# Two heads' keys per PSUM bank, and row spreads by transposition, in a diffusion trunk's kernel

## The chip, the cores and the metric

The kernel runs on one core of one Trainium2 chip. The metric is the device time of one execution in microseconds; before the change three runs took 2082.91, 2083.75 and 2087.36 us, median 2083.75. Everything is float32.

## What is computed

One inference step of a hybrid trunk of two layers, over 512 latent tokens and 128 context tokens, width 1024. A layer is, cut to what matters here:

```
h = rms_norm(x) * (1 + sc1) + sh1
u, vg, ca, cg, rq, rk, rv, rgf, rgb, cq, ckv, kpe = split(h @ w_in)
y_a = spatial gating(u, vg)
y_b = silu(layer_norm(depthwise_conv(ca * sigmoid(cg)), g, b)) @ w_pw      # 256 channels
y_c = bidirectional retention(rq, rk, rv, rgf, rgb)
k, v = ckv @ w_ukv (per head 64 columns of keys, 64 of values) ; k = [k, kpe]   # 4 heads, 768 keys
y_d = softmax(q k^T) v
x = x + g1 * (concat(y_a, y_b, y_c, y_d) @ w_out)
x = x + g2 * expert_choice_ffn(rms_norm(x) * (1 + sc2) + sh2)              # 16 experts
```

g1 and g2 are vectors of 1024 gates, one pair for the latent and one for the context tokens; sc, sh and g come from `silu(c) @ w_mod`.

## The kernel before

Each engine has its program written out by hand and they meet at semaphores. A list STEPS gives the order of the steps of a layer, the same for all engines: input projections of 256 columns each (`in:...`), between them quarters of the modulation product (`mod:...`), latents, queries and keys of the attention (`latents`, `mla_q`, `mla_kv`), the convolution's statistics (`conv_mean`, `conv_var`, `conv_out`), 17 attention blocks (`att:...`), the gates' rows (`rows_g1`), retention, output projection, the choice of tokens by the experts, `rows_g2`, and then the loop over the 16 experts. There is no planner: an instruction stands where STEPS puts it, and waits there.

**PSUM jobs.** Results of TensorE go through three rings of two banks: wide (W, 1024 columns of float32), turned (T) and narrow (N). The lists W_JOBS, T_JOBS and N_JOBS hold the jobs of a layer in order, and a job's place in the list gives its bank (even or odd). `claim` makes TensorE wait until the job two places earlier has been read out, `finish` marks the job done, and `take`, on the instruction that read it out last, frees the bank. `wait` is the reader's wait for a job, `taken` the wait for its having been read out.

**Keys.** `mla_kv` on TensorE (L876 to L890) multiplies, for each of four heads, the head's 64 columns of w_ukv with the transposed latents ckvT of 768 keys, as 512 and 256 columns (L883, L884). The result uses partitions 0 to 63 of a wide bank and half the array's columns. ScalarE copies each head out in one instruction of 64x768 (the helper `out`, L1433, called in L1628) into khT. After the four heads come two jobs of values, v.0 and v.1 (L889), which claim the banks of kh.2 and kh.3; then `turn_q` transposes the queries (the helper `transposes`, L786). ScalarE's copies of v.0 and v.1 and of the turned queries follow the keys' in order, and then the projection `in:u` begins on TensorE (L827).

**Spreads.** In three places a column of values, one per partition, has to become a row that every partition holds. The kernel takes the column as weights, broadcast along the free dimension to 128x128, and multiplies it with the identity: each product gives 128 columns.

- `conv_var` (L914 to L927): five products at L926 spread the convolution's inverse deviation crstd over 640 tokens; VectorE multiplies with it (L1964), ScalarE applies SiLU (L1641) and only then does the softmax of the next attention blocks (L1532).
- `rows_g1` (L1021 to L1029): for latent and context tokens eight products each at L1028; ScalarE copies each 128x1024 job out (L1433). The last attention blocks follow: transposed probabilities of block 15 (L786), their copies by VectorE (L1997) and ScalarE (L1433), and the values (L990).
- `rows_g2` (L1205 to L1218): eight products at L1210 for the latent tokens' gates, then eight products of 32 columns at L1217 for the context tokens'. Ahead of them stand the small transpositions of the experts' tables (L1200, L1202); behind them a spare product (L1416) and the transposition of the first expert's rows (L1229), which POOL gathers from HBM with an indirect DMA (L2405) once the tables are out.

**Experts.** SP issues all weight loads. Each expert needs 12 MB of weights in a ring of 12 slots; expert 0 is loaded during the output projection, and a slot is loaded anew for expert 1 when TensorE has used it (semaphore s_gu_used, raised in `context_gate_up`, L1246).

The lines of a spread, as they stand in `rows_g1`:

```
for k in range(KD):
    ins = mm(o[:, k * P:(k + 1) * P], modT[:, 2 * KD + k, s:s + 1].broadcast_to([P, P]), ident, start=True, stop=True)
W.finish(ins)
```

The functions that the change touches:

Of the kernel before, what the change touches and what calls it, by code (L numbers as in the profile page):

```python
# [24 lines left out]
P = 128  # L25
D = 1024
KD = D // P
# [111 lines left out]
for _s in STEPS:  # L139
    _k, _, _a = _s.partition(":")  # L140
    if _k == "mod":
        for _w, _i in mod_steps(*map(int, _a.split("-"))):
            N_JOBS += [f"modc.{_i}"] if _w == "cols" else [mod_job(_i)] if mod_job(_i) else []
    elif _k == "modc":
        N_JOBS += [f"modc.{_a}"]
    elif _k == "norm1":
        W_JOBS += [f"{_k}.w{i}" for i in range(2)]
        T_JOBS += [f"{_k}.{i}" for i in range(4, KD + 2)]
    elif _k == "in":
        W_JOBS += ["mla_a.s", "mla_a.p", "mla_b"] if _a == "mla" else [f"{_a}.s", f"{_a}.p"] if _a in TOKEN_MAJOR else [f"{_a}.0", f"{_a}.1"]  # L150
        T_JOBS += ["ktok.0", "ktok.1", "ktok.p"] if _a == "rk" else []
    elif _k == "latents":
        T_JOBS += ["cq.0", "cq.1", "cq.p", "ckv.0", "ckv.1", "kpe.0", "kpe.1"]
    elif _k == "mla_q":
        W_JOBS += ["q.0", "q.1", "q.2"]
        T_JOBS += [f"qh.{h}" for h in range(HEADS)] + ["qh.p"]
    elif _k == "mla_kv":
        W_JOBS += [f"kh.{h}" for h in range(HEADS)] + ["v.0", "v.1"]
    elif _k == "mix":
        W_JOBS += ["mix.0", "mix.1"]  # L160
    elif _k == "conv_mean":
        W_JOBS += ["mean"]
    elif _k == "conv_var":
        N_JOBS += ["var"]
        W_JOBS += ["cstd"]
    elif _k == "conv_out":
        W_JOBS += ["pw.0", "pw.1"]
    elif _k == "att":
        W_JOBS += [f"s.{_a}"]
    elif _k == "rows_g1":  # L170
        W_JOBS += ["g1.s", "g1.p"]
    elif _k == "retention":
        N_JOBS += [f"kv.{t}" for t in range(NT)]
        N_JOBS += [f"rs.{_t}.{_h}" for _t in range(NT) for _h in range(2)]
        T_JOBS += [f"ro.{_t}.{_h}" for _t in range(NT) for _h in range(2)]
        T_JOBS += ["yc.0", "yc.1", "yc.p"]
    elif _k == "out":
        W_JOBS += [f"o.{_t}" for _t in (CTX, *range(TS))]
        T_JOBS += [f"xt.{_t}.{_h}" for _t in (CTX, 0, 1) for _h in range(2)] + ["afft.p"]
        T_JOBS += [f"xt.{_t}.{_h}" for _t in (2, 3) for _h in range(2)]  # L180
        N_JOBS += ["lg.p", "lg.s"]
    elif _k == "router_bias":
        N_JOBS += ["bias.r", "bias"]
    elif _k == "choose":
        T_JOBS += ["afft.s"]
    elif _k == "tables":
        T_JOBS += ["tables"]
    elif _k == "rows_g2":
        W_JOBS += ["g2.s", "g2.p"]
    if _k in ("att", "att_end"):  # L190
        for _i in [int(_a)] if _k == "att" else range(NBLOCK, ATT_STEPS):
            if weighed_at(_i) is not None:
                N_JOBS += [f"pv.{weighed_at(_i)}"]
            if turned_at(_i) is not None:
                T_JOBS += [f"pt.{turned_at(_i)}"] + ([f"pt.{turned_at(_i)}b"] if turned_at(_i) < NBLOCK - 1 else [])
# [136 lines left out]
def build(nc, io):  # L332
    ctx = ExitStack()
    with ctx:
# [397 lines left out]
        def _(pe):  # L732
# [143 lines left out]
            def mla_kv(l):  # L876
                wukv = par("wukv", HEADS, 2, NOPE)
                T.taken(pe, l, "ckv.0")
                T.taken(pe, l, "ckv.1")
                for h in range(HEADS):  # L880
                    W.claim(pe, l, f"kh.{h}")
                    o = bank(W, f"kh.{h}", NOPE)
                    mm(o[:, 0:512], wukv[:, h, 0, :], ckvT[:, 0:512], start=True, stop=True)  # L883
                    W.finish(mm(o[:, 512:NKEY], wukv[:, h, 0, :], ckvT[:, 512:NKEY], start=True, stop=True))  # L884
                for j, tiles in enumerate(((0, 1, 2, 3), (4, 5))):
                    W.claim(pe, l, f"v.{j}")
                    o = bank(W, f"v.{j}")
                    for n, t in enumerate(tiles):
                        ins = mm(o[:, n * GW:(n + 1) * GW].rearrange("p (h d) -> p h d", h=HEADS), ckvT[:, t * P:(t + 1) * P], wukv[:, :, 1, :], start=True, stop=True)  # L889
                    W.finish(ins)  # L890
# [23 lines left out]
            def conv_var(l):  # L914
                pe.wait_ge(s_csq, l + 1)
                N.claim(pe, l, "var")
                o = bank(N, "var")
                for t in range(NT):
                    for c in range(NG):
                        ins = mm(o[:, t:t + 1], csq[:, c, t * P:(t + 1) * P], mean_w[:, 0:1], start=(c == 0), stop=(c == NG - 1))  # L920
                N.finish(ins)
                pe.wait_ge(s_crs, l + 1)
                W.claim(pe, l, "cstd")
                o = bank(W, "cstd")
                for t in range(NT):
                    ins = mm(o[:, t * P:(t + 1) * P], crstd[:, t:t + 1].broadcast_to([P, P]), ident, start=True, stop=True)  # L926
                W.finish(ins)  # L927

            def conv_out(l):
# [91 lines left out]
            def rows_g1(l):  # L1021

                N.taken(pe, l, "modc.2")
                for s, job in ((1, "g1.s"), (0, "g1.p")):
                    W.claim(pe, l, job)
                    o = bank(W, job)
                    for k in range(KD):
                        ins = mm(o[:, k * P:(k + 1) * P], modT[:, 2 * KD + k, s:s + 1].broadcast_to([P, P]), ident, start=True, stop=True)  # L1028
                    W.finish(ins)  # L1029

            def retention(l):
# [173 lines left out]
            def rows_g2(l):  # L1205
                N.taken(pe, l, "modc.5")
                W.claim(pe, l, "g2.s")
                o = bank(W, "g2.s")
                for k in range(KD):
                    ins = mm(o[:, k * P:(k + 1) * P], modT[:, 5 * KD + k, 1:2].broadcast_to([P, P]), ident, start=True, stop=True)  # L1210
                W.finish(ins)
                W.claim(pe, l, "g2.p")
                o = bank(W, "g2.p")
                for j in range(QW // P):
                    for q in range(4):
                        col = modT[:, 5 * KD + q * (QW // P) + j, 0:1].broadcast_to([P, STRIP])
                        ins = mm(o[q * STRIP:(q + 1) * STRIP, j * P:(j + 1) * P], col, ident, start=True, stop=True)  # L1217
                W.finish(ins)  # L1218
# [209 lines left out]
        def _(act):  # L1428
# [132 lines left out]
            for l in range(DEPTH):  # L1561
                for s in STEPS:
# [61 lines left out]
                            src = bank(W, f"q.{j}").rearrange("p (t n) -> p t n", t=2)[:, 0:n, 0:HEADS * QK]  # L1624
                            out(W, l, f"q.{j}", qtok[:, 2 * j:2 * j + n, :], src)
                    elif kind == "mla_kv":
                        for h in range(HEADS):
                            out(W, l, f"kh.{h}", khT[0:NOPE, h, :], bank(W, f"kh.{h}", NOPE)[:, 0:NKEY])  # L1628
                        for j, n in enumerate((4, 2)):
                            out(W, l, f"v.{j}", vall[:, 4 * j:4 * j + n, :], bank(W, f"v.{j}")[:, 0:n * GW].rearrange("p (t n) -> p t n", t=n))  # L1630
                        for h in range(HEADS):
# [901 lines left out]
```

## Time and profile before

| what | value |
|---|---|
| runs | 2082.91, 2083.75, 2087.36 us |
| profiled execution, span | 2081.3 us |
| time around the span of that execution | not shown by the page |
| TensorE (PE) busy | 1946.8 us, 94% |
| TensorE weight loads (PEld) | 1084.3 us, 52% |
| VectorE (DVE), ScalarE (ACT), GpSimd (POOL) busy | 533.9, 450.5, 160.5 us |
| mean granted TensorE clock | 0.965 of full speed |
| HBM | 256 GB/s over the span, 380 to 398 in the expert slices |

The profile is of one execution. A float32 product stands in it as two MATMUL records (and two LDWEIGHTS), a transposition as one: L1028 has 64 records for 2 layers times 2 jobs times 8 products. A record's duration contains its way through the array, so the cost of one in a run of many is the length of the run divided by their number. Times are counted from the span's start; layer 0 goes to about 1050 us, layer 1 from there.

### The profile page before, as it was taken

The numbers are of one execution on the slowest core, as the hardware profiler recorded it, in microseconds if no ns is written. First come the engines' busy times: TensorE is split into PE (matmuls) and PEld (weight loads), VectorE is DVE, ScalarE is ACT, GpSimd is POOL, SyncE is SP. The second block draws the span as 40 slices with busy tenths as digits, with TensorE's granted clock in tenths as the row PEclk, the third lists the DMA queues.
The fourth block names the chain that finished last, engine by engine and source line by source line (L and its number), as shares of the span: only waits on it lengthen the run. The fifth ranks groups of instructions, "written<-read, shape, count | busy, mean of one in ns | idle before, by whom it ended". The sixth has DMA issues, their size and how long they took to land.

```text
span 2081.3 us, 36417 instructions
## 1 busy us (share of the span) xinstructions
PE 1946.8 (94%) x14936; PEld 1084.3 (52%) x14936; DVE 533.9 (26%) x1187; ACT 450.5 (22%) x947; POOL 160.5 (8%) x140
## 2 busy tenths in 40 slices
PE   4999999996999999999989999989699999999996
PEld 3756677882444434343365657778544344434342
DVE  1157123533101111111131932253511111111013
ACT  3132232221211111121132214332221121212112
POOL 0000001100111010101000000020010101111110
PEclk8999999996999999999999999999799999999998
DMA  8313122347999999999934122214559999999996
GB/s 311 102 43 122 41 82 85 115 169 271 381 385 395 388 390 393 389 394 390 398 132 139 41 83 81 81 62 194 214 211 392 390 393 389 394 386 397 385 397 240
DMA packets 172887, 532.98 MB, mean 256 GB/s; under 512 B 17296, under 2 KB 50192, under 8 KB 172560
## 3 DMA queue, kind: packets, MB, share of 16 engines
q1 hardware_dynamic: 155248, 493.53, 61.5%
q0 software_dynamic: 11712, 22.29, 4.9%
q10 hardware_dynamic: 5856, 16.16, 2.0%
q8 instruction: 52, 0.85, 0.2%
q14 instruction: 19, 0.16, 0.0%
HBM read 506.59 MB, written 25.33 MB: 256 GB/s over the span
## 4 chain that ended last, share of the span: by engine, by line
PE 66%; DMA 15%; SPq 9%; DVE 5%; issue 4%; ACT 1%; DVEq 0%; ACTq 0%
PE wide L1238 12%; DMA ring<-w_up 12%; PE wide L837 9%; PE wide L827 8%; SPq L644 7%; PE wide L1118 6%; PE wide L1246 6%; PE narrow L1269 6%; PE wide L1282 3%; DMA ring<-w_down 2%; PE turned L786 2%; PE narrow L758 1%; PE wide L954 1%; DMA ring<-w_mod 1%; PE narrow L990 1%
## 5 line engine op out<-in xcount | busy, mean ns | idle before, releaser
L1238 PE MATMUL wide<-ring,ht 128*64 128x512 f32 x2048 | 454.1, 599 | 9.4 <-DMA ring<-w_up 4.8
L1238 PEld LDWEIGHTS wide<-ring,ht 128*64 128x64 f32 x2048 | 143.6, 138 | 304.6 <-issue 278.3
L1269 PE MATMUL narrow<-ring,ht 128*64 128x512 f32 x1024 | 234.3, 599 | 2.3 <-DMA ring<-w_down 2.3
L1246 PE MATMUL wide<-ring,ht 128*32 128x256 f32 x4096 | 234.3, 380 | 0.0
L2202 DVE TENSOR_TENSOR ht<-ht,wide 128x512 f32<-128x512 f32 x64 | 35.5, 555 | 679.6 <-ACT ht L1760 459.2
L837 PE MATMUL wide<-stream,ht 128*128 128x256 f32 (+1 forms) x960 | 195.2, 365 | 3.5 <-DVE ht L1861 3.5
L837 PEld LDWEIGHTS wide<-stream,ht 128*128 128x128 f32 x960 | 171.3, 192 | 26.0 <-issue 5.0
L1246 PEld LDWEIGHTS wide<-ring,ht 128*32 128x32 f32 x4096 | 126.5, 110 | 108.2 <-issue 31.3
L827 PE MATMUL wide<-ht,stream 128*128 128x128 f32 (+1 forms) x640 | 176.3, 437 | 0.0
L1760 ACT ACTIVATE ht<-wide 128x512 f32<-128x512 f32 x32 | 19.1, 597 | 622.7 <-PE wide L1238 622.7
L2408 POOL DMA_INDIRECT moe_sums<-ht x60 | 93.3, 1554 | 712.2 <-DVE ht L2219 637.0
L827 PEld LDWEIGHTS wide<-ht,stream 128*128 128x128 f32 x640 | 96.9, 193 | 73.4 <-issue 73.4
L1269 PEld LDWEIGHTS narrow<-ring,ht 128*64 128x64 f32 x1024 | 67.6, 136 | 121.5 <-issue 114.4
L1282 PE MATMUL wide<-ring,ht 128*32 128x256 f32 x2048 | 117.6, 381 | 0.0
L1118 PE MATMUL wide<-stream,xn_yt 128*128 128x256 f32 x480 | 115.4, 397 | 1.6 <-ACT xn_yt L1499 1.6
L1433 ACT ACTIVATE ring<-wide 128x640 f32<-128x640 f32 (+7 forms) x56 | 40.1, 721 | 288.9 <-PE wide L837 158.7
L1118 PEld LDWEIGHTS wide<-stream,xn_yt 128*128 128x128 f32 x480 | 93.6, 199 | 15.3 <-ACT xn_yt L1433 2.1
L1936 DVE SCALAR_TENSOR_TENSOR ring<-ring,param_cols 128x670 f32<-128x670 f32 x120 | 99.4, 907 | 0.0
L1282 PEld LDWEIGHTS wide<-ring,ht 128*32 128x32 f32 x2048 | 63.1, 110 | 65.6 <-issue 27.5
L1752 ACT ACTIVATE ht<-turned,mod_cols,scale 128x64 f32<-128x64 f32 (+1 forms) x256 | 74.0, 393 | 7.2 <-PE turned L1229 6.7
L2219 DVE SCALAR_TENSOR_TENSOR ht<-narrow,ht 128x512 f32<-128x512 f32 x32 | 24.0, 751 | 185.3 <-PE narrow L1269 185.3
L2210 DVE TENSOR_SCALAR ht<-turned,scale,mod_cols 128x64 f32<-128x64 f32 (+1 forms) x256 | 60.9, 311 | 17.2 <-PE turned L1229 17.2
(283 smaller groups left out, 1549.9 us busy)
## 6 DMA issues: line engine op xcount, KB each, us to landing
ring<-w_gate SPq DMA_DIRECT2D x256, 512.0 KB, 12.3
ring<-w_up SPq DMA_DIRECT2D x256, 512.0 KB, 14.2
ring<-w_down SPq DMA_DIRECT2D x128, 1024.0 KB, 19.9
stream<-w_mod SPq DMA_DIRECT2D x38, 1024.0 KB, 5.4
stream<-w_in SPq DMA_DIRECT2D x20, 1024.0 KB, 7.4
ring<-w_mod SPq DMA_DIRECT2D x10, 1024.0 KB, 18.8
stream<-w_out SPq DMA_DIRECT2D x6, 1024.0 KB, 7.4
moe_sums<-x ACTq DMA_DIRECT2D x10, 512.0 KB, 5.5
```

Source lines behind the costliest of these rows:

```text
L644: sp.dma_start(ring[:, k, i, :], src.rearrange("l e p n -> (l e p) n")).then_inc(s_slot[k], 16)
L827: ins = mm(o[:, lo:hi], w[:, k, c * P:(c + 1) * P], hT[:, k, lo:hi], start=(k == 0), stop=(k == KD - 1))
L837: ins = mm(o[:, n * width:(n + 1) * width], src[:, k, t * P:(t + 1) * P], w[:, k, 0:width], start=(k == 0), stop=(k == KD - 1))
L1118: ins = mm(bank(W, f"o.{t}")[:, u * GW:(u + 1) * GW], yT[:, k, t * P:(t + 1) * P], out_weights[u][:, k, :], start=(u % 2 == 0 and k == OTH ...
L1238: ins = mm(psW[h * 64:(h + 1) * 64, 0, w * HALFW:(w + 1) * HALFW], xT[:, k, 0:CAPS], ring[:, k, w, h * HALFW:(h + 1) * HALFW], start=(k == ...
L1246: ins = mm(psW[q * STRIP:(q + 1) * STRIP, 1, w * QW:(w + 1) * QW], xT[:, k, CAPS:SLOTS], ring[:, k, w, q * QW:(q + 1) * QW], start=(k == 0 ...
L1269: ins = mm(psN[c * 64:(c + 1) * 64, 0, :], hmT[:, j, h_ * 64:(h_ + 1) * 64], ring[:, KD + k // 2, k % 2, c * HALFW:(c + 1) * HALFW], start ...
L1282: ins = mm(psW[q * STRIP:(q + 1) * STRIP, 1, HALFW:HALFW + QW], hmpT[:, j, q_ * STRIP:(q_ + 1) * STRIP], ring[:, KD + k // 2, k % 2, q * Q ...
L1752: ins = A(xT[:, k, lo:lo + n], bank(T, job)[:, k * GROWS + lo:k * GROWS + lo + n], ACT.Identity, scale=A2[:, k, s_:s_ + 1], bias=modT[:, 3 ...
L1936: ins = V.scalar_tensor_tensor(cacc[:, c, :], src, w[:, c, k:k + 1], cacc[:, c, :], ALU.mult, ALU.add)
L2210: ins = V.tensor_scalar(xT[:, 4 + k, lo:lo + n], bank(T, job)[:, k * GROWS + lo:k * GROWS + lo + n], A2[:, 4 + k, s_:s_ + 1], modT[:, 3 * ...
L2408: Q.indirect_dma_start(dst, bass.IndirectOffsetOnAxis(tables[:, j, e:e + 1], 0), src, None, compute_op=ALU.add).then_inc(s_added, 16)
```

## The change

Four edits. The keys of two heads go into one wide bank, head 2c in partitions 0 to 63 and head 2c+1 in 64 to 127, their products issued alternately; ScalarE reads each half out with an instruction of its own, the second into partitions 0 to 63. The three spreads with 128 output partitions are issued as transpositions of the broadcast column. The products of L1217 stay.

```diff
-        W_JOBS += [f"kh.{h}" for h in range(HEADS)] + ["v.0", "v.1"]
+        W_JOBS += [f"kh.{c}" for c in range(NG)] + ["v.0", "v.1"]
...
-                for h in range(HEADS):
-                    W.claim(pe, l, f"kh.{h}")
-                    o = bank(W, f"kh.{h}", NOPE)
-                    mm(o[:, 0:512], wukv[:, h, 0, :], ckvT[:, 0:512], start=True, stop=True)
-                    W.finish(mm(o[:, 512:NKEY], wukv[:, h, 0, :], ckvT[:, 512:NKEY], start=True, stop=True))
+                for c in range(NG):
+                    W.claim(pe, l, f"kh.{c}")
+                    o = bank(W, f"kh.{c}")
+                    for lo, hi in ((0, 512), (512, NKEY)):
+                        for f in range(2):
+                            ins = mm(o[f * NOPE:(f + 1) * NOPE, lo:hi], wukv[:, NG * c + f, 0, :], ckvT[:, lo:hi], start=True, stop=True)
+                    W.finish(ins)
...
-                    ins = mm(o[:, t * P:(t + 1) * P], crstd[:, t:t + 1].broadcast_to([P, P]), ident, start=True, stop=True)
+                    ins = nc.tensor.transpose(o[:, t * P:(t + 1) * P], crstd[:, t:t + 1].broadcast_to([P, P]), ident)
...
-                        ins = mm(o[:, k * P:(k + 1) * P], modT[:, 2 * KD + k, s:s + 1].broadcast_to([P, P]), ident, start=True, stop=True)
+                        ins = nc.tensor.transpose(o[:, k * P:(k + 1) * P], modT[:, 2 * KD + k, s:s + 1].broadcast_to([P, P]), ident)
...
-                    ins = mm(o[:, k * P:(k + 1) * P], modT[:, 5 * KD + k, 1:2].broadcast_to([P, P]), ident, start=True, stop=True)
+                    ins = nc.tensor.transpose(o[:, k * P:(k + 1) * P], modT[:, 5 * KD + k, 1:2].broadcast_to([P, P]), ident)
...
-                        for h in range(HEADS):
-                            out(W, l, f"kh.{h}", khT[0:NOPE, h, :], bank(W, f"kh.{h}", NOPE)[:, 0:NKEY])
+                        for c in range(NG):
+                            W.wait(act, l, f"kh.{c}")
+                            for f in range(2):
+                                ins = A(khT[0:NOPE, NG * c + f, :], bank(W, f"kh.{c}")[f * NOPE:(f + 1) * NOPE, 0:NKEY], ACT.Identity)
+                            W.take(ins, f"kh.{c}")
```

## Rows read from the trace of the kernel before

**Rows 1.** The page: busy us, share of the span, records
```profile
PE 1946.8 (94%) x14936; PEld 1084.3 (52%) x14936; DVE 533.9 (26%) x1187; ACT 450.5 (22%) x947; POOL 160.5 (8%) x140
```
**Rows 2.** The page: chain that ended last, by engine
```profile
PE 66%; DMA 15%; SPq 9%; DVE 5%; issue 4%; ACT 1%; DVEq 0%; ACTq 0%
```
**Rows 3.** Stretches of the expert loop: busy times, clock, DMA share, GB/s
```profile
520.00:730.00 210.00, 210.00 (x1942) 87.74 (x1936) 27.19 (x82) 36.42 (x88) 24.37 (x18) 1.00 1.03 387
```
**Rows 4.** The chain around layer 0's keys: start us, us, what
```profile
127.34 1.00 PE wide L883 x2
128.34 0.43 PE wide L884 x2
...
132.64 1.94 PE wide L889 x8
...
134.60 2.00 ACT ring L1433 x3
```
**Rows 5.** The chain in the expert loop, records and loads merged
```profile
571.84 13.88 PE wide L1238 x64
```
**Rows 6.** Timeline, layer 0: one of four copies of keys, ScalarE
```profile
128.81 0.80 ACT L1433 ACTIVATE ring<-wide 64x768 f32<-64x768 f32 x1 [0.94 <-PE wide L884]
```
**Rows 7.** The chain at transpositions, layer 1, and records of L798 (ns, minimum first)
```profile
1060.62 1.90 PE wide L798 x16
...
1067.40 1.94 PE turned L786 x8
...
L798 PE MATMUL wide<-const_cols,xn_yt x32: 272/375/447, 18.0 to 1062.2; 128*128 128x128 f32 x32
```
**Rows 8.** The chain and ScalarE's timeline around g1's spread, layer 0
```profile
336.69 3.77 PE wide L1028 x32
...
341.41 0.27 ACT L1433 ACTIVATE ring<-turned 128x128 f32<-128x128 f32 x1
341.78 1.31 PE narrow L990 x20
```
**Rows 9.** The chain at g2's spread, layer 1
```profile
1509.17 3.71 PE wide L1210 x16
...
1514.95 0.48 PE turned L1229 x4
```
**Rows 10.** Timeline and chain around crstd's spread, layers 0 and 1
```profile
230.07 1.79 PE L926 MATMUL wide<-const_cols,stats 128*128 128x128 f32 x10 [0.58 <-DVE stats L1962]
231.90 1.49 DVE L1964 TENSOR_TENSOR ring<-ring,wide 128x1280 f32<-128x1280 f32 x1 [1.89 <-PE wide L926]
237.62 2.35 PE L990 MATMUL narrow<-ring 128*64 128x128 f32 x20 [1.78 <-issue]
...
1253.92 1.66 PE wide L926 x10
```
**Rows 11.** Stretches of 1 us, clock third from last: a fall, two rises
```profile
230.00:231.00 1.00, 0.93 (x7) 0.93 (x8) 0.02 (x1) 1.00 (x1) 0.00 (x0) 0.94 1.09 388
...
234.00:235.00 1.00, 1.00 (x6) 0.78 (x6) 0.93 (x3) 1.00 (x2) 0.00 (x0) 0.85 0.00 0
...
1070.00:1071.00 1.00, 1.00 (x7) 0.60 (x5) 0.19 (x1) 0.47 (x2) 0.00 (x0) 0.72 0.00 0
```
**Rows 12.** The chain at g2's spread, layer 0
```profile
493.43 5.30 issue
498.73 1.32 PE turned L1229 x8
```
**Rows 13.** One tile: the gather of layer 1's first rows, POOL
```profile
L2405 POOL DMA_INDIRECT xn_yt<-moe_rows,ht x1: 957/957/957, 1511.0 to 1511.0; - x1
DMA to landing us min/median/max: 3.9/3.9/3.9
```
**Rows 14.** Stretches behind g1's spread, layers 0 and 1
```profile
340.00:347.00 7.00, 5.04 (x63) 4.19 (x62) 2.07 (x5) 2.04 (x5) 0.00 (x0) 1.00 0.34 113
...
1362.00:1371.00 9.00, 6.78 (x96) 5.74 (x97) 2.07 (x5) 2.52 (x8) 0.00 (x0) 1.00 0.27 89
```

## The prediction

> **What bounds the kernel now.** I read the page first for the balance, then the chain of waits for what ends last in each stage, and only then the stages that the change touches. The page says TensorE: busy for 94% of the span, no other engine above 26% [rows 1]. The chain agrees, 66% of it is TensorE, and adds 15% DMA and 9% SP's issues [rows 2]. These two lie in the expert loops. There the DMA engines are at a share of 1.03 while TensorE has no gap either [rows 3]: from the moment when expert 0 frees its first slots, the loop is the loading of a fixed number of bytes, and it ends a fixed time after that moment. So two questions decide what an edit is worth: does it bring TensorE's chain forward in the dense part of a layer, and does that reach the first product of expert 0? Between the keys and the experts I see transfers ordered by what TensorE has used, no idle DMA wait of TensorE, and VectorE's long convolution ending well ahead of its reader; a gain there should be handed on whole. Microseconds below are per layer unless said otherwise, and there are two layers.
>
> **Keys.** A head costs 0.86 us for 512 columns and 0.43 for 256, 1.29 together, the first 0.14 more [rows 4], and four heads 5.16. The two records of the 512 take 430 ns each although they use half the array's columns. In the expert loop the same form, issued for two halves alternately, gives 64 records of 512 columns (32 products) in 13.88 us, 217 ns each [rows 5]. So two halves do run beside each other, and two heads should cost 1.29: TensorE saves 2.58. ScalarE takes part of it back. It begins at 128.81 and needs some 0.74 for each of four copies (0.80 recorded [rows 6], less the overlap of neighbours), so it frees the bank of kh.0 at about 130.3; kh.1 is through at 130.06, so v.0 starts some 0.3 to 0.4 late. v.0 then takes 1.94 and ScalarE's copy of it starts at about 132.45 where it started at 134.60 [rows 4]. What follows (copies, turned queries, the next projection) is a chain behind that copy: **2.15 us** gained. Bounds: nothing, if the halves don't overlap (v.0's copy then starts where it did), and 2.58 if ScalarE were no limit. The copies from partitions 64 to 127 into 0 to 63 have no row; I price them like [rows 6], at worst double, which frees kh.0 0.8 later and costs that much of the 2.15. I take 2.15, since [rows 5] is the same form of product. Late next is ScalarE.
>
> **The price of a transposition.** Sixteen take 1.90 at full clock and eight 1.94 at half: 119 and 243 ns [rows 7] (the 16 stand behind products at full clock, the 8 behind idling). A spreading product takes 3.77/16 = 236 ns at full clock [rows 8] and 3.71/8 = 464 at half [rows 9]. A transposition is one record where the product is two, so half the price is what I expect. No row has a transposition with a broadcast operand; bounds are 119 and 236, and I take 119, as the products of [rows 8] read such columns at the speed of their two records.
>
> **crstd.** VectorE starts 1.83 after the first record in layer 0, and the run takes 1.66 in layer 1 [rows 10]. In layer 0 the clock fell from 2.4 to 1.2 GHz within the run: 0.94 over its first microsecond puts the fall at 230.9 [rows 11]. Five transpositions take 4 x 0.119 and the last one's record, 0.27 [rows 7]: 0.75, done ahead of such a fall. VectorE then starts 1.08 and 0.91 earlier. SiLU, the softmax and the values wait in line behind it: TensorE stands idle 1.78 us ahead of L990 [rows 10], so the gain passes on. **2.0 us for both layers**; bounds 0 at a product's price and 2.0.
>
> **g1.** TensorE: 16 x (236-119) = 1.87. The turned probabilities of the last block and their copy move with it; but ScalarE's second copy of gates (1.0 each for 1024 columns, by the 0.80 for 768 [rows 6]) now ends at about 339.7 and its copy of block 15 (0.27) at 340.0, and L990 needs that. It would start at 340.1 where it started at 341.78 [rows 8]: **1.7 us**. Late next is ScalarE again. Bounds 0 and 1.87.
>
> **g2.** Eight transpositions at half clock save 3.71-1.94 = 1.77 of TensorE's time [rows 7, 9], and I count nothing of it. In layer 0 TensorE waits 5.30 afterwards for the first expert's rows [rows 12]. In layer 1 the gather starts at 1511.0 and lands 3.9 later, 1514.9, and TensorE starts at 1514.95 [rows 9, 13]. The cover is the gather, released by the tables ahead of the spread; were it gone, 1.77 would be gained. There is even something to lose. In layer 1 L1229 runs at full clock (0.48 for four records, where eight took 1.32 in layer 0 [rows 9, 12]), behind the spread's activity; with a shorter spread and more idling it should run at half, and I put a **loss of 0.5 us** in layer 1. ScalarE's copies of these gates lie in the same cover.
>
> **Sum.** 2 x 2.15 + 2.0 + 2 x 1.7 - 0.5 = 9.2 us. The page gives the profiled execution's span alone, 2081.3; the runs' median is 2.5 above it, and I carry that over: 2072.1 of span, **2074.5** of time. The clock's falls between the keys and the experts lie where the work happens to be thin, and with every stage 2 to 7 us earlier they will lie otherwise. The spell of half clock that began at 230.9 ended at 234.3 (0.85 over that microsecond [rows 11]): 3.4 us, at most 1.7 lost or given back by one such spell; I allow 3 in all to each side.
>
> **A rule that speaks against it.** Behind g1's 16 products the clock stays at 1.00 [rows 14], and the rows say that transpositions can serve as well: in layer 1 a run of nothing but transpositions began at half clock [rows 7] and in its course the clock rose (0.72 over the microsecond from 1070 [rows 11], still within such a run). The Trainium skill's page "TensorE: Matmul & The Clock Gate", Part 4, says that transposes don't count as TensorE being busy, so that full clock does not engage for them. By that rule the spreads would stop holding the clock. By it the time would be the first rival's, 2077.9, and by the rows 2074.5. The trace doesn't agree: the rise in [rows 11] came with transpositions alone. No row tells whether they hold a clock as well as products do.
>
> **Rivals.**
>
> *Transpositions hold the clock less than products.* The clock falls behind g1's spread in both layers. For a spell as long as the one above, 3.4 us, what follows runs at half speed: L990 takes 2.35 as in [rows 10] for 1.31 [rows 8], the turned blocks and row sums some 0.7 more, 1.75 in all, as much as g1 gains. 2074.5 + 3.4 = 2077.9. For it: a stretch of 1.9 us of single records in place of 3.77 of double ones, and idling around it. Against: the rise of [rows 11]. Chance 0.17. The Trainium skill's page "TensorE: Matmul & The Clock Gate", Part 4, would have it so.
>
> *The halves of the array don't overlap for keys*, or ScalarE's shifted copies take the gain: 2074.5 + 4.3 = 2078.8. Against: [rows 5]. Chance 0.09.
>
> *A transposition of a broadcast column costs what the product does.* Then the change does only the keys: 2083.75 - 4.3 = 2079.5. Against: [rows 7]. Chance 0.08.
>
> *The clock falls with the first spread and stays down until the output projection*, and expert 0 starts cold: slower than before. Price: 5.04 us of TensorE's work behind g1 in layer 0 and 6.78 in layer 1 [rows 14], now at full clock, would take twice that, 11.8 more; one more spell at half clock at crstd and one at expert 0 in each layer, 4 x 1.7 = 6.8. Together 18.6 against 9.7 gained: 2083.75 - 9.7 + 18.6 = 2092.7. It decides from 9.7 us on, about 19 us more at half clock. The rise in [rows 11] speaks against it. Chance 0.04.
>
> **How the numbers follow.** My forecast has 0.62 and its own range is 2071.5 to 2077.5. To hold 8 in 10 the range takes in the weaker clock and most of the keys' rival: 2070.0 to 2080.0. A measurement of this kernel tells about 0.2% from no change, 4.2 us, so faster is below 2079.6 and slower above 2087.9. Faster: nearly all of the forecast (0.60), most of the weaker clock (0.14), half and more of the keys' rival (0.06) and less than half of the spreads' (0.03): 0.83. Slower: 0.04. Between: 0.13.
>
> **What would show it.** Keys: four records of 512 columns in about 0.9 us, where two took that, v.0's copy by ScalarE 5.1 us after the first key record instead of 7.3. Spreads: half the records, 0.6 us in crstd's and 1.9 in g1's, VectorE's L1964 0.8 after its first. L990 behind g1 3.4 after the spread's first record, where it was 5.1. Ahead of the experts only an idle wait that grew by 1.8 in layer 0, with the gather as its end. The expert loops as long as before, to 1 us. Wrong I would be if the granted clock behind g1 fell to 0.50 for such a spell or more, if the key records took 430 ns each, or if the expert loops changed their length.

## The result, and the profile after

Five runs of the changed kernel took 2071.93 to 2077.11 us, median 2073.98; the kernel before, on the same chip, had a median of 2082.91. The ratio is 0.9955 (95%: 0.9943 to 0.9967), which is 9.4 us less; the medians lie 8.9 apart. The forecast was 2074.5. The profiled execution took 2072.48 us, 2.2 of them around its span of 2070.3 (the forecast had carried over 2.5); the span before was 2081.3, so the two profiles lie 11.0 apart. Of the runs below, one execution of the keys alone took 4751.92 us, for no reason that the record shows, and its ratio leaves that one out. Lines in the changed kernel: keys L885, values L891, keys' copies L1632, crstd's spread L928, VectorE's product with it L1969, g1's L1030, g2's L1212, values of attention L992, first expert's rows L1231.

The page of the changed kernel, busy times and the chain by engine:

```profile
PE 1930.2 (93%) x14878; PEld 1070.2 (52%) x14878; DVE 533.8 (26%) x1187; ACT 450.6 (22%) x947; POOL 160.7 (8%) x140
...
PE 65%; DMA 15%; SPq 9%; DVE 5%; issue 4%; ACT 1%; DVEq 0%
```

TensorE has 58 records fewer and is busy 16.6 us less [rows 1]. That is more than the span lost, so part of its saving lies where nothing waits for it.

**Keys**, layer 0, timeline of TensorE, then of ScalarE (start us, us, engine, line, operation; in brackets the idle time before and its releaser):

```profile
124.38 2.80 PE L885 MATMUL wide<-ring,param_cols 128*64 128x512 f32 x16
127.62 2.86 PE L891 MATMUL wide<-param_cols,ring 128*128 128x256 f32 x12 [0.44 <-ACT ring L1632]
...
125.93 3.28 ACT L1632 ACTIVATE ring<-wide 64x768 f32<-64x768 f32 x4 [0.96 <-PE wide L885]
129.65 1.52 ACT L1435 ACTIVATE ring<-wide 128x1024 f32<-128x1024 f32 x2 [0.44 <-PE wide L891]
```

Sixteen records take 2.80 us from the first one's start to the last one's end, where four heads took 5.37 (5.16 without the way through the array of the last one [rows 4]): two halves run beside each other. TensorE then stands 0.44 for ScalarE, and v.0's copy begins 129.65 - 124.38 = 5.27 after the first key record, where it was 7.3. The four copies start 0.81 to 0.83 apart and last 0.80 to 0.81 each, those out of the upper half no longer than the others.

**crstd**, layer 0, timelines of TensorE and VectorE, and layer 1, TensorE:

```profile
226.78 1.22 PE L928 MATMUL wide<-const_cols,stats 128*128 128x128 f32 x5 [0.58 <-DVE stats L1967]
227.79 1.92 PE L956 MATMUL wide<-ring 96*128 96x512 f32 x2
...
228.03 1.49 DVE L1969 TENSOR_TENSOR ring<-ring,wide 128x1280 f32<-128x1280 f32 x1 [1.31 <-PE wide L928]
...
1247.54 1.33 PE L928 MATMUL wide<-const_cols,stats 128*128 128x128 f32 x5 [0.58 <-DVE stats L1967]
```

VectorE starts 1.25 after the spread's first record, not 0.8: the five transpositions ran at 1.2 GHz, or nearly all of them, in both layers. Stretches of the changed kernel, columns as in [rows 3] (the last three are granted clock, DMA share, GB/s):

```profile
227.00:228.00 1.00, 1.00 (x6) 1.00 (x5) 0.00 (x0) 0.80 (x1) 0.00 (x0) 0.50 1.10 391
1248.00:1249.00 1.00, 1.00 (x6) 1.00 (x5) 0.09 (x1) 0.57 (x1) 0.00 (x0) 0.50 1.09 386
```

The line's records say so too (minimum, median, maximum in ns):

```profile
L928 PE MATMUL wide<-const_cols,stats x10: 363/421/476, 226.8 to 1248.5; 128*128 128x128 f32 x10
L1030 PE MATMUL wide<-const_cols,mod_cols x32: 272/273/323, 332.7 to 1353.7; 128*128 128x128 f32 x32
```

The second line is g1's: a transposition's record lasts 273 ns at 2.4 GHz, and crstd's median of 421 is that of records at 1.2.

**g1**, layer 0, timelines of TensorE and ScalarE:

```profile
332.74 1.96 PE L1030 MATMUL wide<-const_cols,mod_cols 128*128 128x128 f32 x16
334.54 0.71 PE L786 MATMUL turned<-const_cols,ring 128*128 128x128 f32 x5
336.07 1.31 PE L992 MATMUL narrow<-ring 128*64 128x128 f32 x20 [0.82 <-DVE ring L2002]
...
333.87 1.94 ACT L1435 ACTIVATE ht<-wide 128x1024 f32<-128x1024 f32 x2 [2.50 <-PE wide L1030]
335.69 0.28 ACT L1435 ACTIVATE ring<-turned 128x128 f32<-128x128 f32 x1
```

L992 starts 3.33 after the spread's first record, where it was 5.16 by the same timeline (336.62 to 341.78). VectorE's copy of the turned block ends at 335.88, ScalarE's at 335.97: the two are level, and both bound what is left.

The first rival expected the clock to fall behind this spread. Stretches behind it, of the changed kernel in layers 0 and 1, then of the kernel before in layer 0:

```profile
336.00:343.00 7.00, 5.49 (x80) 4.68 (x81) 1.38 (x4) 1.22 (x5) 0.00 (x0) 1.00 0.37 116
1355.00:1369.00 14.00, 11.61 (x162) 9.72 (x162) 4.58 (x17) 3.17 (x12) 0.00 (x0) 1.00 0.25 74
...
343.00:357.00 14.00, 11.93 (x130) 10.10 (x127) 3.72 (x13) 2.92 (x10) 0.00 (x0) 0.64 0.05 13
```

The kernel before has a fall there itself, which [rows 14] just miss: from 346.9, 10.3 us behind the first record of its spread, it stands at 0.50 for 10.2 us. In the changed kernel the clock falls at 343.0, 10.3 behind the spread's first record too, and for 3.4 us only; in layer 1 the kernel before has a fall at 1370.9 and the changed one none. So behind g1 there is less half clock with transpositions, not more.

**g2**, chain of layer 0, then of layer 1 (start us, us, what):

```profile
481.35 1.90 PE wide L1212 x8
483.25 1.01 PE wide L1219 x16
484.26 0.52 PE narrow L1418 x2
484.78 6.80 issue
491.58 1.32 PE turned L1231 x8
...
1498.06 1.90 PE wide L1212 x8
1499.95 1.01 PE wide L1219 x16
1500.97 0.52 PE narrow L1418 x2
1501.48 2.18 issue
1503.67 1.31 PE turned L1231 x8
```

The spread is 1.8 shorter and the idle time behind it is 6.80 instead of 5.30 [rows 12], and in layer 1, where it was 0.54, 2.18. The gather sets L1231's start in both: in layer 1 POOL issues it at 1499.82 and it lands 3.8 later.

**All stages.** The table adds both layers of one profiled execution per kernel, from the first record of one stage to the first record of the next, in us. Those of the experiments stand here too, but for the two with drawn-out spreads. "keys" goes from the first key product to `in:u`, "conv" from the convolution's means to its variance, "crstd" from the spread to the next values (L992), "g1" from the spread to L992, "ret." from retention to the experts' tables, "in" from the first input projection to the keys. "dense" is the whole from the first input projection to the first expert's product, with stages that have no column; "loop" goes from there, in layer 0, to the first input projection of layer 1.

| kernel | in | keys | conv | crstd | g1 | ret. | dense | loop |
|---|---|---|---|---|---|---|---|---|
| before | 155.97 | 22.62 | 66.58 | 14.96 | 10.33 | 276.96 | 899.50 | 570.53 |
| after | 154.78 | 18.48 | 68.29 | 14.06 | 6.66 | 273.68 | 887.65 | 571.86 |
| the change again | 156.65 | 18.47 | 68.26 | 13.82 | 6.66 | 274.53 | 889.24 | 572.40 |
| keys alone | 159.05 | 18.48 | 68.20 | 14.27 | 10.34 | 274.05 | 896.17 | 572.63 |
| g1 alone | 157.77 | 22.62 | 66.57 | 14.52 | 6.66 | 274.81 | 893.10 | 572.20 |
| crstd alone | 157.84 | 22.61 | 66.57 | 13.04 | 10.33 | 270.64 | 891.29 | 573.03 |
| spreads alone | 158.02 | 22.62 | 64.94 | 13.61 | 6.67 | 271.44 | 887.08 | 573.00 |
| spreads again | 157.77 | 22.62 | 66.58 | 13.03 | 6.66 | 271.58 | 888.22 | 571.02 |
| g2 by products | 156.26 | 18.48 | 68.27 | 14.15 | 6.67 | 271.04 | 886.77 | 570.64 |
| keys in turn | 156.37 | 18.52 | 68.29 | 14.13 | 6.66 | 271.28 | 887.44 | 570.56 |
| time refilled | 159.06 | 22.67 | 64.94 | 13.02 | 6.66 | 272.09 | 888.17 | 570.22 |
| wide variance | 157.96 | 18.48 | 68.22 | 13.04 | 6.66 | 274.43 | 890.64 | 572.34 |

Read down a column: keys and g1 have two values each, to 0.05 us, and change with the edit alone. The others change with spells of half clock: conv is 32.47 a layer without one and 34.1 with one, and "in" of layer 0, which no edit can reach, is 76.64 in the changed kernel without half clock and 79.33 in the kernel before with 5.45 us of it. Of the 11.0 between the two profiles, keys give 4.14, g1 3.67 and crstd 0.90, together 8.7. The rest, 2.3, is the balance of the spells (in and ret. 4.5 less, conv 1.7 more, and smaller ones) and of the loop, 1.3 longer.

### The profile page after: what moved, and what is told of

It is laid out like the page before. It is cut to its first block, busy times and chain, and to the rows that moved or that the text cites. A ratio compares the mean times of both kernels' runs of the same rounds, so it can differ in the third digit from the quotient of the medians.

```text
span 2070.3 us, 36301 instructions
## 1 busy us (share of the span) xinstructions
PE 1930.2 (93%) x14878; PEld 1070.2 (52%) x14878; DVE 533.8 (26%) x1187; ACT 450.6 (22%) x947; POOL 160.7 (8%) x140
## 4 chain that ended last, share of the span: by engine, by line
PE 65%; DMA 15%; SPq 9%; DVE 5%; issue 4%; ACT 1%; DVEq 0%
PE wide L1240 12%; DMA ring<-w_up 12%; PE wide L837 9%; PE wide L827 8%; SPq L644 7%; PE wide L1248 6%; PE wide L1120 6%; PE narrow L1271 6%; PE wide L1284 3%; DMA ring<-w_down 2%; PE turned L786 2%; PE narrow L758 2%; PE wide L956 1%; DMA ring<-w_mod 1%; PE narrow L1143 1%
## 5 line engine op out<-in xcount | busy, mean ns | idle before, releaser
L1435 ACT ACTIVATE ring<-wide 128x640 f32<-128x640 f32 (+6 forms) x48 | 33.8, 708 | 277.5 <-PE wide L837 157.7
L1757 ACT ACTIVATE ht<-turned,mod_cols,scale 128x64 f32<-128x64 f32 (+1 forms) x256 | 74.1, 393 | 10.6 <-PE turned L1231 10.2
```

What stands on the lines that cost most here:

```text
L1757: ins = A(xT[:, k, lo:lo + n], bank(T, job)[:, k * GROWS + lo:k * GROWS + lo + n], ACT.Identity, scale=A2[:, k, s_:s_ + 1], bias=modT[:, 3 ...
```

## The experiments

Ratios are to the kernel before on the same chip, and gains in us are worked out from them; one per mille is 2.08 us.

**Keys alone.** The changed kernel with all three spreads as products.

```diff
-                    ins = nc.tensor.transpose(o[:, k * P:(k + 1) * P], modT[:, 5 * KD + k, 1:2].broadcast_to([P, P]), ident)
+                    ins = mm(o[:, k * P:(k + 1) * P], modT[:, 5 * KD + k, 1:2].broadcast_to([P, P]), ident, start=True, stop=True)
```

(and likewise for crstd and g1.)

> The change with its three spreads turned back into products: only the keys are paired. By my sum (the halves of the array work beside each other, ScalarE then limits) v.0's copy starts 5.2 to 5.3 us after the first key record instead of 7.3, and the time is 4.2 us below the kernel before, about half of what the change gives. By the rival that the halves don't overlap, or that ScalarE's copies from the upper partitions take the gain, it is within 1 us of the kernel before, and the change's gain is the spreads' alone.

Measured: 2079.0 us over 12 runs (2078.46 without that one), 0.9982 (0.997 to 0.9993). The stage is 2.07 shorter in each layer, and the total is shorter by 3.7, with an interval of about 2.4 to each side.

**Spreads alone.** The kernel before with the three transpositions and its own keys; run twice, the second time beside a repeat of the whole change.

```diff
-                    ins = mm(o[:, t * P:(t + 1) * P], crstd[:, t:t + 1].broadcast_to([P, P]), ident, start=True, stop=True)
+                    ins = nc.tensor.transpose(o[:, t * P:(t + 1) * P], crstd[:, t:t + 1].broadcast_to([P, P]), ident)
```

(and likewise for g1 and g2.)

> The kernel before with the three spreads as transpositions and its keys as they were. By my sum 2.0 (crstd, both layers) + 3.4 (g1) - 0.5 (g2) = 4.9 us below the kernel before, or 4.1 with crstd's run at half clock as the changed kernel's trace has it. Together with the keys alone this should add up to the whole change's 9. By the rival that transpositions let the clock fall behind g1's spread, 1 to 2 us below.

Measured: 2072.37 us, 0.9946 (0.9933 to 0.9959).

> The kernel before with the three spreads as transpositions, again. The stage from the convolution's mean to its variance takes 32.5 us in one layer at least (no spell at half clock), and the stage from crstd's spread to the next values 6.5 at full clock or 7.0 to 7.1 at half.

Measured: 2072.97 us, 0.9951 (0.9936 to 0.9967).

> The changed kernel unaltered, beside the spreads alone on one chip. By the sum of the stages (keys 2.07 us a layer) it is 4.1 us below the spreads alone. By the theory that the keys' gain is partly given back, because with the work 2 us earlier a spell at half clock (1.6 us) falls between the convolution's mean and its variance in every layer instead of in some, the difference is 1 to 3 us, and that stage takes 34.1 us in both layers here.

Measured: 2073.27 us, 0.995 (0.9932 to 0.9968). The spreads alone are as fast as the whole change. Three expectations missed: the spreads alone gained 11.2 and 10.2 us where 4.9 was the sum, the parts (3.7 and 11.2) add up to more than the whole (9.4), and the repeated change is neither 4.1 nor 1 to 3 us below the spreads. The spreads' stages give what the sum says (crstd 1.4 and 1.9, g1 3.7 in the two profiles); most of the surplus is in retention, 5.5 and 5.4 shorter than in the profile of the kernel before, which no line of the edit reaches. Keys alone gain, keys on top of the spreads don't show; what takes their 4.1 us is taken up below.

**g1 alone and crstd alone.** One transposition put into the kernel before, each as in the diff above.

> The kernel before with g1's spread alone as transpositions. By my sum L990 starts 3.3 to 3.4 us after the spread's first record instead of 5.1 in both layers, the granted clock stays at 1.00 behind it, and the time is 3.4 us lower. By the rival of the weaker clock it falls to 0.50 within some microseconds behind the spread and the time is that of the kernel before.

Measured: 2080.69 us over 12 runs, 0.9987 (0.9974 to 1.0), 2.7 us less, where 3.4 was expected; the stage is 1.83 shorter in each layer. In layer 0 the clock fell 8.9 us behind the spread's first record, for 10.2 us, as in the kernel before.

> The kernel before with crstd's spread alone as transpositions. VectorE's multiplication starts 0.75 us after the spread's first record at full clock and about 1.25 at half, instead of 1.8, and L990 the same amount earlier; the time 1.2 to 2.0 us lower, at the edge of what can be measured. If the softmax were not waiting for it, nothing.

Measured: 2075.98 us over 9 runs, 0.9973 (0.996 to 0.9986). Here the five transpositions ran at full clock. Timelines of TensorE and VectorE, layer 0:

```profile
229.12 0.76 PE L926 MATMUL wide<-const_cols,stats 128*128 128x128 f32 x5 [0.58 <-DVE stats L1962]
...
229.92 1.49 DVE L1964 TENSOR_TENSOR ring<-ring,wide 128x1280 f32<-128x1280 f32 x1 [0.85 <-PE wide L926]
```

VectorE starts 0.80 after the first record and the stage takes 6.52, against 7.55 and 7.41 before. So the term of the sum, 1.0 a layer, holds at full clock; at 1.2 GHz, as in the changed kernel, 0.3 to 0.6 of it is left. The total gained more, 5.6 us, than the stage's 1.9, and more than expected; the retention stages of this profile are 6.3 shorter than in the one of before, which has the longest of the table, though no line of the edit reaches them. What differs there is the clock. The same stretch as above, layer 0, in this kernel:

```profile
343.00:357.00 14.00, 12.04 (x151) 10.44 (x151) 6.05 (x22) 3.02 (x10) 0.00 (x0) 1.00 0.05 11
```

It is 1.00 here and 0.64 in the kernel before.

**The halves in turn.** The first head's two products, then the second's, instead of alternating.

```diff
-                    for lo, hi in ((0, 512), (512, NKEY)):
-                        for f in range(2):
+                    for f in range(2):
+                        for lo, hi in ((0, 512), (512, NKEY)):
```

> The change, but within a bank the first head's 512 and 256 columns are issued before the second head's, so that neighbours in the queue are halves only once. If the gain comes from neighbouring halves, the 16 key records take 3.9 us or more instead of 2.7 (of a bank's 2.57 us of records alone, only the 256 of one head and the 512 of the other overlap, 0.43), and v.0's copy comes 0 to 1.3 us later a layer, the time up to 2.5 us above the change. If pairing in one bank were what counts, no difference.

Measured: 2070.49 us, 0.9942 (0.9929 to 0.9956), not told apart from the change. Timeline of TensorE, layer 0:

```profile
126.07 2.85 PE L885 MATMUL wide<-ring,param_cols 128*64 128x512 f32 x16
129.32 2.86 PE L891 MATMUL wide<-param_cols,ring 128*128 128x256 f32 x12 [0.40 <-ACT ring L1632]
```

2.85 against 2.80, and not the 3.9 expected if neighbours in the queue were what counts. The overlap needs two heads in different halves of the array; it does not need them issued by turns. The trace shows how: of the first bank's eight records the four of 512 columns start at 126.07 to 126.57 and the four of 256 only from 126.98, though the first head's 256 were issued ahead of the second head's 512. The second head's products start beside the first head's.

**g2 by products.** The changed kernel with L1212 as a product.

> The change with g2's spread turned back into products. By my sum the gather covers it: the same time within 1 us, TensorE's idle wait ahead of the first rows shorter by 1.8 us in layer 0 and 1.7 in layer 1, L1229's form of record at full clock again in layer 1 (0.75 us for eight instead of 1.30), which would give 0.5 us back. If the spread did lie on the path, 1.8 us a layer more than the change.

Measured: 2073.23 us, 0.9957 (0.9942 to 0.9973). Chain of layer 1:

```profile
1500.24 1.01 PE wide L1219 x16
1501.25 0.52 PE narrow L1418 x2
1501.77 0.47 issue
1502.25 1.32 PE turned L1231 x8
```

The idle time is 0.47 here and 2.18 with transpositions: g2's transpositions move time from work into waiting. The expected 0.5 us from L1231 did not come back. L1231 runs at half clock with products in this kernel (1.32 for eight records); in the kernel with the spreads alone it runs at full clock with transpositions. Chain of that one, layer 1:

```profile
1499.81 1.28 PE wide L1210 x6
1501.09 1.01 PE wide L1217 x16
1502.10 0.39 PE narrow L1416 x2
1502.50 2.45 issue
1504.94 0.48 PE turned L1229 x4
```

So it is not the form of g2's spread that decides the clock of L1231, and the 0.55 that it lost in layer 1 is not the transpositions' price. Each of these is one profile.

**Do transpositions hold the clock?** Two kernels with g1's and g2's spreads drawn out to some 8 to 11 us, one by transpositions (each job six times over), one by products (three times).

```diff
-                    for k in range(KD):
+                    for k in [k for _ in range(6) for k in range(KD)]:
```

(g2 likewise; in the other kernel `range(3)` and `mm` in place of the transposition.)

> The change with each transposition of g1's and g2's spread issued six times over: 96 in a row behind the attention (at full clock before), 48 at g2 (at half clock before). If transpositions hold and raise the clock as products do, g1's run takes 96 x 0.119 = 11.4 us at a granted clock of 1.00 throughout, and g2's run begins at 0.243 each and ends at 0.119 each, 8 us rather than 11.7. If they don't count for the clock, it falls to 0.50 within g1's run, which takes 15 to 20 us, stays down behind it, and g2's run keeps 0.50 and takes 11.7. Time: 2 x (11.4 - 1.9) = 19 us above the change at g1 by the first, 27 to 36 by the second; at g2 up to 5 us a layer lie under the wait for the gather in layer 0.

> The same places with products issued three times over: 48 at g1, 24 at g2, runs about as long as in the kernel with repeated transpositions. By every theory g1's run takes 48 x 0.236 = 11.3 us at a granted clock of 1.00, and g2's begins at 0.464 each and ends at 0.236 each with the clock risen after some microseconds. It is the measure for the transpositions: where both granted clocks behave alike, a transposition is worth as much to the clock as a product.

Measured: 2092.39 us (1.004, 1.0025 to 1.0056) and 2092.17 (1.0037, 1.002 to 1.0053). g1's run of layer 0 in the two, timeline of TensorE, transpositions first:

```profile
334.37 10.69 PE L1030 MATMUL wide<-const_cols,mod_cols 128*128 128x128 f32 x96
```

```profile
334.31 10.98 PE L1030 MATMUL wide<-const_cols,mod_cols 128*128 128x128 f32 x96
```

96 transpositions in the one, 96 records of 48 products in the other: 111 ns per transposition, 229 per product. Stretches of the kernel with transpositions, columns as in [rows 3] (the last three are granted clock, DMA share, GB/s), g1 first, then g2, which began at half clock:

```profile
336.00:337.00 1.00, 1.00 (x12) 1.00 (x10) 0.00 (x0) 0.00 (x0) 0.00 (x0) 1.00 1.09 376
344.00:345.00 1.00, 1.00 (x11) 1.00 (x10) 0.00 (x0) 0.00 (x0) 0.00 (x0) 1.00 0.00 0
...
497.00:498.00 1.00, 1.00 (x7) 1.00 (x6) 0.00 (x0) 0.00 (x0) 0.00 (x0) 0.50 1.08 442
498.00:499.00 1.00, 1.00 (x10) 1.00 (x9) 0.00 (x0) 0.00 (x0) 0.00 (x0) 0.87 1.01 406
499.00:500.00 1.00, 1.00 (x11) 1.00 (x10) 0.00 (x0) 0.00 (x0) 0.00 (x0) 1.00 1.09 315
```

The same of the run with products, g2:

```profile
493.00:494.00 1.00, 1.00 (x7) 1.00 (x7) 0.00 (x0) 0.00 (x0) 0.00 (x0) 0.50 1.01 410
494.00:495.00 1.00, 1.00 (x8) 1.00 (x8) 0.00 (x0) 0.00 (x0) 0.00 (x0) 0.65 1.03 422
495.00:496.00 1.00, 1.00 (x12) 1.00 (x11) 0.00 (x0) 0.00 (x0) 0.00 (x0) 1.00 1.06 385
```

Either run keeps a clock of 1.00 through 10 us, and either one brings it from 0.50 to 1.00 in its course, 5.6 us after its first record with transpositions and 5.8 with products. The Trainium skill's page "TensorE: Matmul & The Clock Gate", Part 4, says that full clock does not engage for transposes, as they don't count as activity in the same way. These traces disagree, with 96 float32 transpositions at 1.00 from end to end.

**Is it the 2 us that bring a spell of half clock?** In the stage from the convolution's means to its variance the clock falls in 16 of the 16 layers of the eight kernels whose keys take 9.24 us (change, its repeat, keys alone, in turn, g2 by products, wide variance, the two drawn-out ones), and in 4 of the 10 of the five kernels with their keys as before, 11.3. So I kept the paired keys and gave the time back: the second pair's products issued three times over.

```diff
-                    for lo, hi in ((0, 512), (512, NKEY)):
+                    for lo, hi in ((0, 512), (512, NKEY)) * (1 + 2 * c):
```

> The change with the second pair of heads' key products issued three times, so that TensorE spends on keys the 5.2 us that it spent before. By the theory that only the moment of the work counts for the spells, this kernel is the spreads alone: keys' stage 11.3 us, the stage from the mean to the variance 32.5 us in some layers, and its time that of the spreads alone. If pairing in itself brought the spell, the stage takes 34.1 in both layers and the time is 2 us above the spreads alone.

Measured: 2073.75 us, 0.9957 (0.9942 to 0.9971). Keys take 11.33, no spell in this stage in either layer (2 x 32.47), crstd at full clock in both (13.02). With this kernel it is 4 layers of 12 where the keys take 11.3, and 16 of 16 where they take 9.24. crstd's transpositions go with it: at full clock in 7 of 8 layers with keys of 11.3, in 1 of 12 with 9.24 (the wide variance below left out). The total can be told neither from that of the spreads alone nor from that of the change, whose keys are 4.2 us shorter. Stretches of this kernel, then of the change's repeat, same chip, same work (L956 after an idle stretch), within the first layer's stage from the means to the variance:

```profile
204.00:205.00 1.00, 0.94 (x2) 0.49 (x3) 0.01 (x1) 0.90 (x3) 0.00 (x0) 1.00 0.00 0
205.00:208.00 3.00, 3.00 (x25) 2.75 (x24) 1.64 (x4) 1.05 (x3) 0.00 (x0) 1.00 0.03 5
```

```profile
202.00:203.00 1.00, 1.00 (x2) 0.49 (x3) 0.00 (x0) 0.73 (x2) 0.00 (x0) 0.69 0.00 0
203.00:206.00 3.00, 3.00 (x15) 2.74 (x14) 1.64 (x4) 1.02 (x3) 0.00 (x0) 0.53 0.00 0
```

The idle time of some 2 us before it is the same, and the work from `in:u` on is the same; only its distance from what TensorE did earlier differs, by 2 us.

**A busier variance product.** The products before crstd's spread (L922) have one column each; here they have 96, of which ScalarE reads one, to see whether the spread then runs at full clock.

```diff
-                        ins = mm(o[:, t:t + 1], csq[:, c, t * P:(t + 1) * P], mean_w[:, 0:1], start=(c == 0), stop=(c == NG - 1))
+                        ins = mm(o[:, t * 96:(t + 1) * 96], csq[:, c, t * P:(t + 1) * P], mean_w[:, 0:96], start=(c == 0), stop=(c == NG - 1))
```

> The change with the ten products of the convolution's variance giving 96 equal columns in place of one; they are bound by their weight loads (20 records in 2.34 us, 117 ns each), so their run should stay at 2.34. If it is their thinness that lets the clock fall at crstd's spread, the granted clock stays at 1.00 there, the stage from the spread's first record to the next values takes 6.5 us in both layers instead of 7.0 to 7.1, the next stage no spell either (22.06 instead of 23.7), and the time is 1 to 3 us below the change. If the clock falls for the waits around it, nothing changes.

Measured: 2076.53 us, 0.9958 (0.9941 to 0.9975). The spread does run at full clock in both layers (stage 6.52 each) and the products cost 0.08 a layer more. So crstd's two stages together are 1.0 shorter than the change's. The stage behind it is at half clock in layer 0 (23.67, where 22.06 is its length without), but so it was in the change (23.65), and the spell in conv is there too. The total doesn't move: the dense part is 890.64, 3.0 longer than the change's, and "in", which lies ahead of these products in a layer, is 3.2 longer. One profile can't tell whether a busier product ahead helps for good.

## Why the prediction came out right

The time was 0.5 us from the forecast, and no rival came true. The operations cost what the sum says, but that its total came out was in part luck: alone, the spreads gained twice what they were given (10.2 and 11.2 for 4.9), and the keys on top of them nothing that shows (for 4.3). The terms, one by one:

- **Keys, 2.15 a layer:** 2.07 in every kernel that has the edit and doesn't refill its time. ScalarE is the limit behind them, as said.
- **g1, 1.7 a layer:** 1.83. Transpositions with a broadcast operand take 118 ns here (1.89/16) and 111 in the long run, where I took 119. ScalarE's last copy came 0.1 sooner than I put it, level with VectorE's.
- **crstd, 2.0 for both:** 0.9 between the two profiles. The duration at full clock was right (6.51 or 6.52 in ten layers of six kernels), the step that failed is "done ahead of such a fall": the spread came at half clock in both layers of the change. The size of a term was off by 1.1, through the clock, not through the operation.
- **g2, nothing:** right, and hidden where I said, under the gather (idle 5.30 to 6.80). The loss of 0.5 in layer 1 did occur in the changed kernel (0.55), but its cause was not the shorter spread: with products it occurs as well, and in the kernel with the spreads alone, which has the transpositions, it doesn't.
- **"A gain there should be handed on whole":** this step failed for the keys. Each stage's gain is there, but the spells move. Without the keys' edit, dense takes 887.08, 888.22 and 888.17 with the spreads; with it, 887.65, 889.24, 886.77 and 887.44: means of 887.8 in both groups, though the second has 4.1 less in the keys' column. On the means conv goes from 65.5 to 68.3, crstd from 13.2 to 14.0 and ret. from 271.7 to 272.6, and stages not in the table lose 1.8 more; "in" gives 2.3 back. From the first key product to g1's spread, both layers, the trace's clock stands at 0.50 for 6.83, 10.24 and 6.83 us in the first group and for 17.07, 13.65, 17.06 and 17.06 in the second: 8.2 more on the means, and half of that is the 4.1 of the keys. Keys alone could keep their gain: there this time is 13.65 us, the same as in the kernel before.
- **The same from all executions.** Each run has its mean granted clock on record. It is 0.9678 over the 16 runs of the first group and 0.9656 over the 23 of the second; the times are level, 2073.4 and 2073.0. Within the runs of one kernel, 0.001 of clock goes with 1.24 us (0.12 to each side, over 139 runs). With that, at one clock, the keys are worth 3.3 us on top of the spreads (about 1 to each side), the spreads 5.0 against the kernel before, and the whole change 8.2, near the sum's 9.2. This is an estimate, but it doesn't rest on single profiles: the operations gave what was forecast, and the clock took the keys' part back.
- **Expert loops as long as before, to 1 us:** 1.3 longer in the profile, but 570.2 to 573.0 over all kernels without order by the edit: a scatter that I should have put at 3.
- **The allowance of 3 us for spells** to each side was too small for the terms, though the total didn't need it. Terms too high by 1.1 (crstd) and about 4 (keys) stand against spells in the kernel before that the sum could not know: the retention stages of its profile are over 2 us longer than in any other row of the table, and its runs have a mean clock of 0.9639, below all but one of the kernels tried. That these met, and the number came out, was luck.

Of the rivals, the one that transpositions don't hold the clock was refuted by the stretches behind g1 and by the two drawn-out kernels, and the other three by the keys' column, by 118 ns, and by g1's records, which ran at full clock behind crstd's at half.

## What to carry to other kernels

A float32 product that only spreads a column is worth issuing as a transposition: it takes half the time on the clock of the moment and kept the clock as well as products did. It pays only where something waits for it, which nothing did at g2. Two products that use half the array each belong in different halves, in whatever order they are issued. In a kernel whose clock falls now and then, a gain of 2 us read from a stage is the gain of that stage only: look at the granted clock of every stage behind it, compare several kernels of the same length before giving a part of the total to one edit, and compare their mean granted clocks along with their times.

## What the hardware showed that I had not expected

Moving a stage by 2 us moved the spells of half clock: 16 of 16 layers against 4 of 12 (0 of 2 with the time refilled, 4 of 10 with the keys as before). What sets the moment is not settled here. Two half-array products of one bank overlapped although one head's 512 and 256 columns were issued ahead of the other's (2.85 against 2.80 us for 16 records). And the gather of the first expert's rows landed 3.8 us after its issue in layer 1 and 8.2 in layer 0; the DMA engines' share over these stretches was 0.39 and 1.03. That landing, not TensorE, decides what g2's spread is worth.
